# Hybrid decoder step in fp32: the tile of 128 tokens rebuilt, with channel-wise projections, two buffers for the transposed input, and the row roots on another engine

## What is computed

```python
def hybrid_layer(x, c, ...):
    h = rmsnorm(x, norm_pre) * (1.0 + scale_m) + shift_m
    qa, ka, va, ga, pb, gb, xc, gc = split(h @ w_in)     # 2880 columns
    ya = swa_banded(rope(qa), rope(ka), va, sinks) * silu(ga)   # window 128, 8 heads of 64
    yb = rwkv7_time_mix(pb, gb, ...)     # token shift, decay, delta rule over 64 x 64 states
    yc = rglru_mix(xc, gc, ...)          # width-4 convolution, two gates, linear scan
    y = concatenate([ya, yb, yc]) @ w_out
    return x + gate_m * rmsnorm(y, norm_post)
```

## Time and profile before

| | us |
|---|---|
| Time, median of 3 | 3261.7 (3260.98 to 3263.45) |
| The profiled execution, its own time | 3271.33 |
| Its span | 3269.5 |
| Granted TensorE clock, mean | 0.961 |
| One tile of the steady loop | 90.47, some 92.0 |
| DVE at the end of a tile: two scalings of the output, residual add | 0.75 + 0.74 + 1.23 |
| DVE then: four copies of the state's v | 1.19 |
| DVE: the convolution (L1328, L1332, L1335) | 0.60 + 1.91 + 0.17 |

### The profile page before, as it was taken

The page is one execution under the profiler, slowest core; times in us unless marked ns, Lnnn a source line. Parts: engine busy times, 40 slices in busy tenths (PEclk is TensorE's granted clock), DMA queues, the critical chain, the costliest instruction groups (busy, mean ns, idle before and its releaser), DMA issues.

```text
span 3269.5 us, 62255 instructions
## 1 busy us (share of the span) xinstructions
PE 3017.4 (92%) x24404; PEld 1852.7 (57%) x24404; DVE 1750.7 (54%) x4385; ACT 1429.8 (44%) x3055; POOL 0.2 (0%) x4
## 2 busy tenths in 40 slices
PE   4899999999999999998649999999999999999986
PEld 3555556666655555665335555566666655555654
DVE  1455555556555555555414555555566555555554
ACT  0444445445544444544204444454455544445432
POOL 0000000000000000000000000000000000000000
PEclk7999999999999999999769999999999999999996
DMA  9000000000000000000370000000000000000001
GB/s 371 8 20 20 20 20 19 7 20 20 20 13 20 20 20 20 19 7 14 119 289 2 20 20 20 20 19 7 20 20 20 13 20 20 20 20 19 12 9 39
DMA packets 36847, 116.07 MB, mean 36 GB/s; under 512 B 13104, under 2 KB 16304, under 8 KB 36016
## 3 DMA queue, kind: packets, MB, share of 16 engines
q1 hardware_dynamic: 29136, 89.20, 7.8%
q10 hardware_dynamic: 7648, 26.04, 2.1%
HBM read 96.83 MB, written 18.41 MB: 35 GB/s over the span
## 4 chain that ended last, share of the span: by engine, by line
PE 75%; DVE 15%; issue 6%; DMA 2%; ACT 1%; ACTq 0%; DVEq 0%; SPq 0%
PE G L419 37%; PE M L757 14%; PE M L415 5%; PE G L652 4%; DVE small L1367 2%; DMA RB<-in_w_mod 2%; PE M L579 2%; PE M L566 2%; PE G L425 2%; DVE W L1291 1%; DVE RA L1332 1%; DVE Q L1315 1%; PE M L602 1%; PE M L512 1%; PE M L545 1%
## 5 line engine op out<-in xcount | busy, mean ns | idle before, releaser
L419 PE MATMUL G<-w_in,hT 128*128 128x512 f32 (+2 forms) x3072 | 1296.6, 572 | 3.1 <-DVE hT L1212 3.1
L419 PEld LDWEIGHTS G<-w_in,hT 128*128 128x128 f32 x3072 | 571.4, 191 | 552.8 <-issue 474.9
L757 PE MATMUL M<-w_out,yT 128*128 128x512 f32 x1024 | 454.1, 597 | 5.2 <-DVE yT L1446 5.2
L757 PEld LDWEIGHTS M<-w_out,yT 128*128 128x128 f32 x1024 | 191.3, 192 | 223.9 <-issue 223.9
L1224 DVE TENSOR_TENSOR xs<-pB 128x768 f32<-128x768 f32 x32 | 30.7, 959 | 395.8 <-ACT pB L938 395.8
L1315 DVE TENSOR_TENSOR Q<-Q,M 64x256 f32<-64x256 f32 x320 | 133.8, 418 | 119.4 <-PE M L579 115.3
L566 PE MATMUL M<-W 64*64 64x64 f32 x4608 | 163.5, 218 | 7.8 <-DVE W L1291 7.8
L566 PEld LDWEIGHTS M<-W 64*64 64x64 f32 x4608 | 149.4, 135 | 11.3 <-issue 11.3
L630 PE MATMUL M<-kT,stA 64*128 64x256 f32 x512 | 144.3, 402 | 0.0
L652 PE MATMUL G<-Vt,RB 128*128 128x64 f32 x1024 | 127.9, 278 | 0.0
L579 PEld LDWEIGHTS M<-Q,W 64*64 64x64 f32 x2560 | 88.2, 134 | 68.2 <-issue 68.2
(11 more groups left out here) (403 smaller groups left out, 4559.2 us busy)
## 6 DMA issues: line engine op xcount, KB each, us to landing
w_in<-in_w_in SPq DMA_DIRECT2D x2, 11520.0 KB, 33.3
xa<-in_x_prompt SPq DMA_DIRECT2D x16, 512.0 KB, 3.6
RA<-in_w_mod ACTq DMA_DIRECT2D x16, 512.0 KB, 6.3
W<-in_w_mod ACTq DMA_DIRECT2D x16, 512.0 KB, 6.5
w_out<-in_w_out SPq DMA_DIRECT2D x2, 4096.0 KB, 36.7
G<-in_x_prompt SPq DMA_DIRECT2D x16, 512.0 KB, 3.3
x_mid<-RA SPq DMA_DIRECT2D x16, 512.0 KB, 2.8
xa<-x_mid SPq DMA_DIRECT2D x16, 512.0 KB, 3.7
```

Of the source, the lines that this page charges most:

```text
L419: last = mm(out[:, 0:width], hT[:, k, :], Win[:, k, col:col + width], start=k == 0, stop=k == KC - 1)
L757: last = mm(o[:, :], yT[:, k, :], Wout[:, k, 512 * h:512 * h + 512], start=k == 0, stop=k == KC - 1)
```

## The change

- `channels()` is new: blocks of `Win` (128 x 128) are the weights and `hT` moves (128 columns), so r, k, v, the low-rank inputs, xc and gb/gc come out by channels. `channels_rk`, `channels_vw` and the transposes of xc and gb/gc are gone, on PE and on ACT. `ka` and `va` become fills of width 128.
- `hT` has two buffers, and the loop body holds two tiles (`b` = 0, 1), in 7 turns instead of 15; two tiles stand behind it.
- The gate projection gb/gc goes in four parts (`gates(j)`) into the state chain. `gates(0)` waits for `h_hi(n+1)`.
- `x_lo(n+1)` comes behind `multiply(5)`; `x_hi(n+1)` behind `scores(1)`, in `G0` too, and so behind `h_lo(n+1)`; on ACT `h_lo(n+1)` stands behind `exps(0)`, on DVE the scaling (`x_mean`, in place in `xa`) ahead of `maxima(0)` and `h_hi(n+1)` behind `product(5)`. SP's load of the next rows waits for `xT_hi` in place of `xn_ready`.
- The convolution and the LRU gates come early in the tile; the LRU gate products stand inside the q projection. Rotary moves behind the second level of the inverse. The operands of the delta rule and their tables on ACT are made for the next tile, beside `project(1)` (`front`, `decays`, `operands`).
- In `scores` the matmuls of the two halves of the partitions alternate.
- The three square roots of a tile on ACT, with the reciprocals on DVE, become sums and powers on POOL, of 1 to 4 elements per partition.

```diff
-    hT = sb("hT", [P, KC, P])
+    hT = sb("hT", [P, 2, KC, P])
+            def channels(out, H, col, width):
+                for k in range(KC):
+                    last = mm(out[0:width, :], Win[:, k, col:col + width], H[:, k, :], start=k == 0, stop=k == KC - 1)
+                return last
...
                 def x_hi(m):
-                    pe.wait_ge(s["pT0_act"], BEFORE(m))
+                    pe.wait_ge(s["hT_lo"], DONE(m))
...
-                def fill_rk(m):
-                    fill(G0, C_R, 512, range(KC)).then_inc(s["rk_mm"], 1)
+                    for j in range(4):
+                        last = channels(G0[:, P * j:P * j + P], H, C_R + P * j, P)
...
-                    fill(G1, C_V, 448, range(KC)).then_inc(s["vwk_mm"], 1)
+                    for j in range(2):
+                        channels(G1[:, P * j:P * j + P], H, C_V + P * j, P)
+                    channels(G1[:, 2 * P:3 * P], H, C_WA, 64)
+                    fill(G1[:, 3 * P:4 * P], H, C_KA, P, range(KC)).then_inc(s["vwk_mm"], 1)
...
+                    for j in range(2):
+                        channels(G1[:, P * j:P * j + P], H, C_XC + P * j, P)
+                    fill(G1[:, 2 * P:3 * P], H, C_VA, P, range(KC)).then_inc(s["xv_mm"], 1)
+                    pe.wait_ge(s["rk_out"], DONE(n))
+                    fill(G0, H, C_Q, 512, range(0, 6))
+                    pe.wait_ge(s["conv_ready"], DONE(n))
...
                     scores(0, M3, M4).then_inc(s["s0_mm"], 1)
                     multiply(5)
+                    if ahead:
+                        pe.wait_ge(s["q_out"], DONE(n))
+                        x_lo(n + 1)
...
                     scores(1, M0, M1).then_inc(s["s1_mm"], 1)
+                    if ahead:
+                        x_hi(n + 1)
+                    pe.wait_ge(s["q_dve"], STEP(n, 5, 5))
                     right_side(0)
+                    if ahead:
+                        pe.wait_ge(s["hT_hi"], DONE(n + 1))
+                    gates(0)
                     solve(0)
                     pe.wait_ge(s["exp0"], DONE(n))
                     probs(0, M3, M4).then_inc(s["pT0_mm"], 1)
                     next_state(0)
                     outputs(0).then_inc(s["s_mm"], 1)
-                    if ahead:
-                        x_lo(n + 1)
+                    gates(1)
...
+                    gates(2)
+                    gates(3).then_inc(s["gbc_mm"], 1)
...
                     exps(0, M3, M4, s["neg0"], s["es0"], s["exp0"])
+                    if ahead:
+                        h_lo(n + 1, hT[:, 1 - b])
+                    solved(0)
...
+                def x_root(m):
+                    pool.wait_ge(s["x_squared"], DONE(m))
+                    xlink(ts(small[:, 1:2], small[:, 0:1], D * EPS, None, ALU.add))
+                    tt(small[:, 7:8], small[:, 1:2], minus, ALU.pow).then_inc(s["x_root"], 1)
...
                     power_T(5)
+                    if ahead:
+                        x_mean(n + 1)
                     maxima(0, M3, M4, s["s0_mm"], s["neg0"])
                     product(5)
+                    if ahead:
+                        h_hi(n + 1, hT[:, 1 - b])
                     rhs(0)
```

More of the change, by code:

```diff
@@ L47 @@
 LNX_EPS = 64e-5
+ROOT_D = float(D) ** 0.5
 LRU_C = 8.0
@@ new lines, in tile @@
+                    cw, cb = par("cw"), par("cb")
+                    for c in range(2):
+                        last = ts(lu[:, c, :], xcb[:, c, 0:P], cw[:, c:c + 1], cb[:, c:c + 1], ALU.mult, ALU.add)
+                    link(last)
+                    for t in range(1, 4):
+                        for c in range(2):
+                            last = stt(lu[:, c, :], xcb[:, c, t:t + P], cw[:, 2 * t + c:2 * t + c + 1], lu[:, c, :],
+                                       ALU.mult, ALU.add)
+                        link(last)
@@ new lines, in tile @@
+                    cp(xcb[:, :, 0:3], xcb[:, :, P:P + 3]).then_inc(s["conv_ready"], 1)
+                    dve.wait_ge(s["bonus_mm"], DONE(n))
+                    tt(bonv[:, :], G1[:, 0:256], xsv, ALU.mult).then_inc(s["bonus_out"], 1)
+                    dve.wait_ge(s["gA_mm"], DONE(n))
+                    o = CST["mst"][0]
+                    later = cst[:, o:o + 512]
+                    for r, m in zip(half, (M0, M1)):
+                        last = tt(NW[r], m[r, :].rearrange("p (w u c) -> p w u c", w=2, c=CH), over(nstrict[r], 2, U),
+                                  ALU.mult)
@@ new lines, in tile @@
+                    last.then_inc(s["ntn_ready"], 1)
+                    dve.wait_ge(s["ntn_ready"], DONE(n))
+                    tt(Q[:, :, :], NW[:, 0], over(eye[:, :], 1, U), ALU.add).then_inc(s["q_init"], 1)
+                    dve.wait_ge(s["o_ready"], BEFORE(n))
+                    dve.wait_ge(s["gB_mm"], DONE(n))
+                    for r, m in zip(half, (M3, M4)):
+                        mask = later[r, :].rearrange("p (w c) -> p w c", w=2)[:, :, r]
+                        last = tt(G24[r], m[r, :].rearrange("p (u w c) -> p u w c", w=2, c=CH), over(mask, 1, U), ALU.mult)
@@ new lines, in product @@
+                    def product(level):
+                        dve.wait_ge(s["q_mm5"], STEP(n, level, 5))
+                        for r, m in zip(half, HB):
+                            last = tt(Q[r, :, :], Q[r, :, :], m[r, 256:512].rearrange("p (u c) -> p u c", c=CH), ALU.add)
+                        last.then_inc(s["q_dve"], 1)
+                    power_T(1)
+                    dve.wait_ge(s["gC_mm"], DONE(n))
+                    for r, m in zip(half, HB):
+                        last = tt(G3T[r], m[r, 0:256].rearrange("p (u c) -> p u c", c=CH), over(con("mit")[r, r], 1, U),
+                                  ALU.mult)
@@ L1272, in tile @@
+                    last.then_inc(s["gC_ready"], 1)
+                    product(1)
+                    power_T(2)
                     dve.wait_ge(s["q_out"], DONE(n))
@@ L1344, in tile @@
                     power_T(4)
-                    product(4)
-                    if ahead:
-                        x_mean(n + 1)
-                    power_T(5)
                     dve.wait_ge(s["lru_root"], DONE(n))
@@ L1412, in tile @@
                     last.then_inc(s["ytm_ready"], 1)
+                    dve.wait_ge(s["ytm_ready"], DONE(n))
+                    link(tt(Q[:, :, :], ytm, ytm, ALU.mult))
+                    red(small[:, 52:56], Q[:, :, :], AX_X, ALU.add).then_inc(s["y_sums"], 1)
                     dve.wait_ge(s["exp1"], DONE(n))
@@ L1461, in tile @@
                     link.end()
-                for step in (x_mean, x_norm, h_hi, token_shift):
-                    step(l * NT)
-                with dve.Fori(0, NT - 1) as i:
-                    tile(l * NT + i, True)
-                tile(l * NT + NT - 1, False)
+                x_mean(l * NT)
+                h_hi(l * NT, hT[:, 0])
+                token_shift(l * NT)
+                operands(l * NT)
+                with dve.Fori(0, NT // 2 - 1) as i:
+                    tile(l * NT + 2 * i, 0, True)
+                    tile(l * NT + 2 * i + 1, 1, True)
+                tile(l * NT + NT - 2, 0, True)
+                tile(l * NT + NT - 1, 1, False)
                 dve.wait_ge(s["o_ready"], BEFORE((l + 1) * NT))
```

560 lines of the change are left out of this document (250 added, 310 removed).

## The result

The changed kernel takes 3360.6 us (3357.15 to 3365.27, 4 runs), the kernel before 3261.3 on the same chip (3260.91 to 3263.45, 4 runs): 1.0304 of it, with an interval of 1.0286 to 1.0322. It is 99 us slower. The forecast was slower by 45, with 3235 to 3345 as its range, so the direction was right and the size was not.

A forecast was written before the change was run, and what follows sets the result against it. PE, busy in 92% of the span, was taken as the bound. Terms of +0.7 us per tile plus +0.8 for the clock, times 30, gave 45 us on 3271.3; less 9.6 for the median, 3307 us, range 3235 to 3345.

The forecast's parts named there:

- the clock: PE's waits between scores(1) and outputs(0): clock falls in about half of the tiles, +0.8 us per tile (0 to 1.55).
- The tile without a fall: Sum of all terms per steady tile except the clock's: +0.7 us, or +1.1 with slow scores.
- Passes of `channels`: Projections on PE: 240 passes of 128 columns at 0.112 us replace 24.95 us; +1.93 us per tile (+0.7 to +4.8).
- The transposes' -1.5: 13 transpose passes on PE (r/k, v and low-rank, gb/gc, xc) go, 0.11 us each: -1.5 us per tile.
- the +2.4 of the stretch: From multiply(4) to the next step: x_hi waits for h_lo behind exps(0), gates(0) begins at 10.8 us against 8.44.
- The rest of the state chain: After the stretch: x_lo with its wait and x_hi's transposes go, gates add some 0.25 us: -1.1 us per tile.
- The convolution's wait: PE's 0.97 us wait for the convolution ahead of the LRU gates goes: -1.0 us per tile.
- POOL is free for PE: Roots moved from ACT to POOL: in time at 1 us per instruction, so 0 us per tile.
- it nets out: Rival, chance 0.08: passes at 0.107 us (-1.2 per tile) with the clock held, about 3255 to 3268 us.
- The wait comes, the clock holds: Rival, chance 0.18: PE waits as forecast but the clock doesn't fall, 3283 to 3295 us.
- h_lo lands in time: Rival, chance 0.16: h_lo lands before PE needs it at x_hi; 3208 us, or 3145 if scores are also halved.
- Instruction fetch: Rival, chance 0.05: the two-tile loop outgrows what PE holds, each of 12 jumps waits for a fetch, hidden by project(1).

The follow-up runs named there:

- e2: The changed kernel with useless matmuls on PE, eight ahead of x_hi and four ahead of the wait for h_hi: 3294.0 us, 1.0084 of before.
- e4: The changed kernel with the matmuls of scores in their old order, half by half: 3354.9 us, 1.0279 of before.
- e7: The changed kernel with eight useless matmuls on PE ahead of x_hi alone: 3302.3 us, 1.0131 of before.
- e1: The changed kernel with h_lo(n+1) ahead of exps(0) on ACT in place of behind it: 3210.4 us, 0.9823 of before.
- e6: e1 with the matmuls of scores in their old order, half by half: 3252.7 us, 0.9963 of before.
- e5: e1 with DVE's scans behind rhs(0), x_lo ahead of multiply(5), x_hi between the halves of scores(1), seven q passes ahead of LRU gates: 3156.3 us, 0.9684 of before.

## Why the forecast was off, step by step

**The step that failed is the clock.** "I expect the fall in about half of the tiles: +0.8 (0 to 1.55)". It fell in all 30, and cost 2.1 us per tile (93.99 in the changed kernel against 91.87 in `e2`), 64 us in place of 24. The mechanism was right, both numbers in it were too small. How often: the rows of before were read as a place on the edge, three falls in 30, and more waiting as a nudge; but even `e4`, whose waits of 1.51 and 0.85 us are about what the forecast had (1.4 and 1.1), had the fall in every tile. How dear: 1.55 was the price of a fall of 3.4 us at half clock. The trace's record of the clock shows, in the changed kernel's 30 steady tiles, 170.7 us at half clock together: ten falls of 3.4 us and twenty of 6.8, 5.7 in the mean. In the steady tiles of before all three are of 3.4. The upper bound of the term was thus taken from the shorter kind.

**The tile without a fall** was forecast at +0.7 and is 91.56 less 90.47 = +1.1, and +0.3 more on average for the jump. Term by term, at the whole clock, in starts of PE's rows:
- Passes of `channels`: forecast 26.88 us for 240 at 0.112. Long runs keep to it; PE's timeline in `e7`, the 64 of rk and the 32 of xc with what follows each:

```profile
1085.48 7.36 PE L430 MATMUL G<-hT,w_in 128*128 128x128 f32 x64
1092.68 0.60 PE L421 MATMUL M<-cst,stA 128*128 128x128 f32 x4
...
1116.67 3.73 PE L430 MATMUL G<-hT,w_in 128*128 128x128 f32 x32
1120.24 7.10 PE L425 MATMUL G<-w_in,hT 128*128 128x128 f32 x28
```

  That is 7.20 and 3.57, 0.112 a pass. But `gates(0)` and `gates(1)` take 1.98 for 16 each, 0.124 a pass, the upper bound, for groups between blocks of another shape pay at the borders. With `gates(2)` and `gates(3)` 3.67, v, low-rank and ka 7.44, va 1.79, the sum is 27.65, so +2.7 for +1.9. The rule cited of the Trainium skill ("TensorE: Matmul & The Clock Gate", section Back-to-back issue gap), by which the term would have been +39 us, found no support: the long runs are at 0.112.
- The transposes' -1.5 and the +2.4 of the stretch hold. The groups that are gone held PE before for 0.31 + 0.43 + 0.44 + 0.33 = 1.5 us. From `multiply(4)` to `gates(0)` it is 10.86 us, forecast 10.8; `x_hi` begins 8.7 behind, forecast 8.6. Every link was a row of before, and the order of each engine is fixed. The scores ran side by side, so PE's wait is 3.1 and not 1.4, with the same end, as the forecast said it would be.
- The rest of the state chain was forecast at -1.1: from `solve(0)` to the rk fill before takes 11.56 us, and in `e7`, less the three groups of gates in between (1.99 and 3.68), 10.15: -1.4.
- The convolution's wait is gone from 18 tiles, and 0.5 remain in the 12 behind a jump. The forecast put the loop at 0 because the "12 backward jumps stand behind project(1), 6.9 us of queued matmuls". That is PE's side of it; DVE's own fetch behind the jump was not looked at.
- POOL is free for PE, as forecast: the root of the next rows is ready at 992.69, and DVE asks at 994.18. For the output's root DVE begins 1.66 us behind ACT's sum of squares in `e1`, 1.82 in before. One sign of being wrong did come, a POOL instruction of over 1 us: the power of four elements takes 1.04, and DVE waits for it in each tile (43.0 us in 32 waits), but PE doesn't wait for what follows.

```profile
991.82 0.22 POOL L1110 TENSOR_SCALAR small<-small 128x1 f32<-128x1 f32 x1 [29.54 <-ACT RB L899]
992.12 0.57 POOL L1111 TENSOR_TENSOR small<-small,expo 128x1 f32<-128x1 f32 x1
```

**Sum:** 1.1 + 0.3 + 2.1 = 3.5 per tile against a tile of before with the whole clock, 3.36 against the mean of before, which has three falls in it; forecast 1.5. The terms of the whole-clock tile, 2.7 - 1.5 - 1.1 + 2.4 - 1.4, give its 1.1: the passes were put 0.8 too low, and the chain's saving makes up for 0.3 of that. Of the 49 us by which the span grew beyond the forecast (94 for 45), 40 are the clock, 11 this tile and 9 the jumps; 5 that falls cost before already and the 7 of the heads and ends, which the forecast had expected to add time if anything, come off.

**Small slips in its sums,** none of which enters the 3307: PE's work in the stretch without a wait adds up to 8.2 us, not 8.3; slow scores make `maxima(0)` 0.1 later, so the stretch would be 10.9 and not 11.2 (`e4`'s tiles are as long as the changed kernel's); and "it nets out", 0.7 or 1.1 less 1.2 per tile, gives 3247 to 3259, not 3255 to 3268.

**The rivals.** "The wait comes, the clock holds", 3283 to 3295, is what `e2` and `e7` made of the kernel: 3294 and 3302. "h_lo lands in time" has two prices, and both were 45 to 65 us too low: 3208 with the scores as they were is `e6`, 3252.7, and "if scores are also halved", 3145, is `e1`, 3210.4. That `e1` lies near 3208 is chance. Per tile `e1` gains 1.7 us where 3.9 were forecast; left out were the wait for `h_hi`, which stays (0.85), the 0.54 behind the alternating scores, the 0.3 of the jump and the 0.4 of the whole-clock tile, 2.1 together. `e5`, which closes most of these, reaches 3156. Slow POOL didn't come about. Instruction fetch did, but on DVE and not on PE: the guessed 2 us per jump is what DVE's gaps have, and on average all but 0.3 us per tile was covered.

**What the change is worth apart from its one bad order.** The rebuilt tile does more passes than the old one and is still 1.7 us shorter than it (88.89 against 90.63) once PE doesn't have to wait for `exps(0)`. `e1` shows a gain of 1.8% that the changed kernel had given up for two ACT steps in the wrong order, and `e5`, with three more moves, one of 3.2%.

## What to carry to other kernels

A wait that is put ahead of dense work is to be priced twice, as idle time and as the passes behind it at half clock; here 3.1 us of waiting took 5.1 off when it went, and a bound for the clock's part that comes from the falls of the old trace can be too low: there they lasted 3.4 us, here up to 6.8. When the next item's input is prepared inside a chain, look whether its evacuation can stand ahead of whatever on that engine waits for the chain itself: here that one swap was worth 150 us. And before an edit is called worthless, see whether a wait behind it hides it: the alternating scores were worth 0 in one order of ACT and 42 us in the other.

## What the runs showed that I had not expected

- PE given matmuls of no use, 2.05 us of them in each of the tiles' longest waits, was 2% faster (3360.6 to 3294.0 us), the clock whole in all 30 steady tiles.
- Products of the two halves of the partitions that alternate run side by side: eight passes of 256 columns in 1.13 us, as four in the old order. 64 x 64 blocks straight behind them begin 0.54 us late; behind four transposes put in between they don't.
- DVE begins 1.8 to 2.2 us late behind each backward jump of a loop of two tiles, with an instruction packet at the start of the gap, and behind the 28 jumps of the loop of one tile not at all.
- Powers on POOL take 0.57 us for one element per partition and 1.04 for four, so their time grows with so few elements already; a sum of two operands of one element takes 0.44.
